# Thirteen of 31 taps of one channel chunk of a depthwise convolution, moved from VectorE to GpSimd

## The chip, the cores and the metric

The kernel runs on one core of a Trainium2 chip. The metric is device time in microseconds (us) of one execution, the median over several runs. In the profile the engines are called PE (TensorE), DVE (VectorE), ACT (ScalarE), POOL (GpSimd) and SP (SyncE, here a queue of transfers).

## The reference: what is computed

Two networks run one after the other on 256 tokens of width 1024, in float32. The change touches the first one alone, in both of its layers (`DEPTH = 2`). Each layer projects its normed input into three branches, runs the branches, concatenates, projects out, and then goes through a large expert block. The branches:

```python
y_att  = forgetting_attention(q, k, v, log_f)      # 8 heads of 64
y_conv = conformer_conv(proj[..., C0:C1], ...)     # 256 channels
y_rnn  = rglru_block(...)
mixed  = concatenate([y_att, y_conv, y_rnn]); x = x + mixed @ w_out[l]
```

The convolution branch gates its input (`a * sigmoid(gate)`), convolves every channel by itself along the tokens with 31 taps (causal: token t sees t-30 to t), adds a bias, takes a layer norm over the 256 channels of each token, and applies SiLU. The second network needs six modulation vectors per layer, `silu(cond) @ mod_w + mod_b`: 24 MB of weights per layer, of which the kernel computes the products early, in the first network's layers.

## The kernel before, in words

Data lie with features on the 128 partitions and tokens along the free dimension, so the convolution's 256 channels are two chunks c = 0 and 1 of 128 partitions by 256 tokens. Everything of this kind (`yconv`, `ypad`, `sqc`, `cen`, scores, probabilities) lives in one big tile that the profile calls `arena`; the constants, tap weights among them, are in `K`, vectors of scalars in `col`. Every float32 product of the big matrices is done as high and low parts: ACT rounds a weight tile (line 1143), DVE takes the rest (L1613), and PE multiplies. Each engine runs its own program in the order of the code and meets the others by semaphores.

**A layer's mixer on DVE.** While PE projects (20 weight tiles), DVE puts taps 0 to 17 of the convolution, both chunks, between its other work. A tap is one instruction (L1766 in `conv`): the padded input shifted by j times the tap's weight, plus `yconv` so far, written to `yconv`; so each tap of a chunk waits for the tap before it. Then comes the loop over attention heads (h = 0 to 8). For head h DVE adds biases to the scores (L1838, L1840), takes maxima (L1844, L1845), and for head g = h-1 divides ACT's exponentials by their sums (L1850 to L1852, which sets `p_ready`), and then does two taps of both chunks, `taps(18 + 2 * g, 20 + 2 * g)`, four instructions (two in g = 6, where only tap 30 is left). After g = 6 it sets `conv_done`.

**The head loop on PE** (from L706 on). At step h it makes the scores of head h+1, the value product of head h-2 and the transposes of head h-1, the last of which wait for `p_ready`. At h = 1, 3 and 5 it also does modulation blocks 7, 8 and 9 (`mod_block`, L622 on; PE rows `bank<-HA,csp`, 32 matmuls in four pieces of 8). At h = 8 it waits for `conv_done` and sums `yconv` over the channels (`bank<-arena,K`, 4 records of 128x256). DVE, ACT and PE then take turns at the layer norm and SiLU; beside that PE does modulation block 10; and then the out-projection begins, whose first weight tile needs the convolution's output last (a wait for DVE's L1829).

**The modulation weights on POOL.** A block of modulation needs four transfers of 512 KB (48 per layer, numbered j; block b uses j = 4b to 4b+3). POOL issues them in order (L2308) into four slots; transfer j may start when PE has used the piece that lay in its slot, that is piece j-4 (`after(pool, S("mod_mm"), ...)`). So the transfers of block 8 start as the pieces of block 7 are used, and so on. In this stage POOL does nothing else. Later, in the expert block, POOL takes the low parts of some tiles (L2296), and between the networks it adds up squares of the context in three additions of 128x1024, 128x512 and 128x256 (L2317), each of which waits for the one before.

Of the kernel before, what the change touches and what calls it, by code (L numbers as in the profile page):

```python
# [12 lines left out]
ALU = mybir.AluOpType  # L13
# [7 lines left out]
T = 256  # L21
# [3 lines left out]
TAPS, RTAPS = 31, 4  # L25
# [37 lines left out]
MODS = [(0, 7), (7, 10), (10, 12)]  # L63
MOD_HEADS = {1: 7, 3: 8, 5: 9}
MSLOT = 4


U_POOL = 18
# [175 lines left out]
def after(eng, sem, value):  # L244

    if not isinstance(value, int) or value > 0:
        eng.wait_ge(sem, value)  # L247
# [17 lines left out]
def build(nc, wts, mod_d, cst_d, keys_d, mla_d, bias_d, x_d, ctx_d, out_d, stop_after=None):  # L265
    ctx = ExitStack()
    with ctx:
# [5 lines left out]
        def S(name):  # L273

            if name not in sems:
                sems[name] = ctx.enter_context(nc.semaphore(name))
            return sems[name]
# [33 lines left out]
        def k(name, a=0, b=None):  # L311
            at, w = CONST[name]
            return K[:, at + a:at + (w if b is None else b)]
# [20 lines left out]
        cvA, cvG, yconv, cen, sqc = (area(2, T) for _ in range(5))  # L334
        ypad, rpad = area(2, T + TAPS - 1), area(2, T + RTAPS - 1)
# [174 lines left out]
        def _(pe):  # L510
# [137 lines left out]
            for l in range(L):  # L648
# [57 lines left out]
                for h in range(HEADS + 2):  # L706
                    if h + 1 < HEADS:
                        head_scores(h + 1)
                    if h < 2:
                        keep_clock(4 + h, bank[3])  # L710
                    if h >= 2:
                        g = h - 2
                        po, hc = slice(64 * (g % 2), 64 * (g % 2) + 64), g // 2
                        pe.wait_ge(S("pt_ev"), HEADS * l + g + 1)
                        if hc >= 2:
                            pe.wait_ge(S("y_ev"), 4 * l + hc - 1)
                        yb = bank[hc % 2]
                        mm(yb[po, 0:T], vtok[:, 0, g * HD:(g + 1) * HD], PT[g % 2][:, 0:T], True, False)
                        mm(yb[po, P:T], vtok[:, 1, g * HD:(g + 1) * HD], PT[g % 2][:, T:3 * P], False, True)\
                            .then_inc(S("pv_mm"), 1)  # L720
                    if 1 <= h <= HEADS:
                        g = h - 1
                        pe.wait_ge(S("p_ready"), HEADS * l + g + 1)
                        if g >= 2:
                            pe.wait_ge(S("pt_ev"), HEADS * l + g - 1)
                        for i in range(3):
                            m = nc.tensor.transpose(bank[6 + g % 2][:, i * P:(i + 1) * P], Pm[g % 2][:, i * P:(i + 1) * P], ident)
                        m.then_inc(S("pt_mm"), 1)
                    if h in MOD_HEADS:
                        mod_block(l, MOD_HEADS[h])  # L730
                    if h == HEADS:
                        pe.wait_ge(S("conv_done"), l + 1)
                        pe.wait_ge(S("y_ev"), 4 * l + 3)
                        for c in range(2):
                            m = mm(bank[0][:, 0:T], k("ones"), yconv[:, c, :], c == 0, c == 1)
                        m.then_inc(S("ln_sum"), 1)
                    if h == HEADS + 1:
                        pe.wait_ge(S("ln_sq"), l + 1)
                        for c in range(2):
                            m = mm(bank[0][:, 0:T], k("ones"), sqc[:, c, :], c == 0, c == 1)  # L740
                        m.then_inc(S("ln_var"), 1)
# [177 lines left out]
            for l in range(L):  # L919
# [13 lines left out]
                if l == 0:  # L933
                    for i in range(16):
# [9 lines left out]
                        j = i - 3  # L944
# [5 lines left out]
                    for o in range(16):  # L950
# [11 lines left out]
                        if o - 1 in MLA_AT:  # L962
                            j = MLA_AT.index(o - 1)
# [3 lines left out]
                        if o - 3 in MLA_AT:  # L967
                            j = MLA_AT.index(o - 3)
# [51 lines left out]
                else:  # L1020
                    for i in range(24):
# [13 lines left out]
                        j = i - 3  # L1035
# [544 lines left out]
        def _(dve):  # L1580
# [139 lines left out]
            for l in range(L):  # L1720
# [33 lines left out]
                lo(t0 + 5 + LEAD)  # L1754
                dve.wait_ge(S("proj_ev"), N_EV * l + 6)

                def conv(out, src, taps, w, b, span, last):

                    for j in span:
                        for c in range(2):  # L1760
                            if j == 0:
                                last[c] = link(v.tensor_scalar(out[:, c, :], src[:, c, 0:T], w[:, c * taps:c * taps + 1],
                                                               b[:, c:c + 1], ALU.mult, ALU.add))
                            else:
                                dve.wait_ge(S("dve_order"), last[c])
                                last[c] = link(v.scalar_tensor_tensor(  # L1766
                                    out=out[:, c, :], in0=src[:, c, j:j + T], scalar=w[:, c * taps + j:c * taps + j + 1],
                                    in1=out[:, c, :], op0=ALU.mult, op1=ALU.add))
# [3 lines left out]
                dve.wait_ge(S("dve_order"), ends[1])  # L1772
                dve.nop().then_inc(S("xr_ready"), 1)

                def taps(a, b):

                    conv(yconv, ypad, TAPS, k(f"cw{l}"), k(f"cb{l}"), range(a, min(b, TAPS)), ends)

                def gate_bias(i):

# [41 lines left out]
                gate_bias(3)  # L1822
                mod_add(l, *MODS[0])
                dve.wait_ge(S("bc_ev"), 5 * (l + 1))
                def mix_low(p):

                    cs = MIX_PARTS[p]
                    dve.wait_ge(S("h_hi"), SPLITS[f"m{l}"][0] + p + 1)
                    v.tensor_tensor(Hl[:, cs[0]:cs[-1] + 1, XS], mixT[:, cs[0]:cs[-1] + 1, :], Hh[:, cs[0]:cs[-1] + 1, XS],  # L1829
                                    ALU.subtract).then_inc(S("h_out"), 1)  # L1830

                for h in range(HEADS + 1):
                    if h < HEADS:
                        dve.wait_ge(S("att_mm"), HEADS * l + h + 1)
                        if h >= 2:
                            dve.wait_ge(S("att_exp"), HEADS * l + h - 1)
                        s_, b = sc[h % 2], bank[4 + h % 2]
                        v.scalar_tensor_tensor(out=s_[:, 0:P], in0=b[:, 0:P], scalar=cT[:, 0, h:h + 1],  # L1838
                                               in1=biasT[:, h, 0:P], op0=ALU.add, op1=ALU.add)
                        v.scalar_tensor_tensor(out=s_[:, P:], in0=b[:, P:3 * P], scalar=cT[:, 1, h:h + 1],  # L1840
                                               in1=biasT[:, h, P:], op0=ALU.add, op1=ALU.add).then_inc(S("att_sc"), 1)
                        dve.wait_ge(S("att_sc"), HEADS * l + h + 1)
                        nm = col[:, 8 + 2 * (h % 2):10 + 2 * (h % 2)]
                        v.tensor_reduce(nm[:, 0:1], s_[:, 0:P], AXX, ALU.max, negate=True)  # L1844
                        v.tensor_reduce(nm[:, 1:2], s_[:, P:], AXX, ALU.max, negate=True).then_inc(S("att_mx"), 1)  # L1845
                    if h >= 1:
                        g = h - 1
                        dve.wait_ge(S("att_exp"), HEADS * l + g + 1)
                        sm = col[:, 12 + 2 * (g % 2):14 + 2 * (g % 2)]
                        seq(v.reciprocal(sm, sm))  # L1850
                        v.tensor_scalar(Pm[g % 2][:, 0:P], Pm[g % 2][:, 0:P], sm[:, 0:1], None, ALU.mult)
                        v.tensor_scalar(Pm[g % 2][:, P:], Pm[g % 2][:, P:], sm[:, 1:2], None, ALU.mult)\  # L1852
                            .then_inc(S("p_ready"), 1)
                        taps(18 + 2 * g, 20 + 2 * g)
                        if g == 6:
                            dve.wait_ge(S("dve_order"), ends[1])
                            dve.nop().then_inc(S("conv_done"), 1)
                        if g == HEADS - 1:
                            dve.wait_ge(S("ln_sum"), l + 1)
                            for c in range(2):  # L1860
                                m = v.scalar_tensor_tensor(out=cen[:, c, :], in0=bank[0][:, 0:T], scalar=-1.0 / 256,
                                                           in1=yconv[:, c, :], op0=ALU.mult, op1=ALU.add)
                            m.then_inc(S("ln_cen"), 1)
                    if h == 7:
                        mix_low(0)
# [420 lines left out]
        def _(pool):  # L2286
# [16 lines left out]
            for l in range(L):  # L2303
                after(pool, S("acc_done"), l)
                for j in range(4 * MODB):
                    n = 4 * MODB * l + j
                    after(pool, S("mod_mm"), n - MSLOT + 1)
                    pool.dma_start(mslot[n % MSLOT], mod_d[n].rearrange("p (a b) -> p a b", a=4)).then_inc(S(f"mod_in{n % MSLOT}"), 16)  # L2308
                pool.wait_ge(S("h_out"), SPLITS[f"m{l}"][1])
                pool.dma_start(keysT.rearrange("p a b -> p (a b)"), keys_d[l]).then_inc(S("keys_in"), 16)  # L2310
                rests(l)
# [31 lines left out]
```

## Time and profile before

| | |
|---|---|
| median of 3 runs | 3182.95 us (3178.98 to 3203.91) |
| profiled execution | 3179.1 us, its span 3177.3 us |
| granted TensorE clock, mean | 0.993 of full speed |
| PE busy | 3111.9 us, 98% of the span |
| DVE busy | 2145.9 us, 68% |
| ACT busy | 1384.7 us, 44% |
| POOL busy | 253.2 us, 8% |

Span is from the first to the last instruction. Busy shares are means over stages of very different kinds: an engine with 68% over the span can be without a gap in the stage that is changed, and one that is 98% busy can be waiting in it between short matmuls. Layer 0's head loop lies from about 116.4 to 146.8 us from the start of the span, layer 1's 1016.7 us later.

### The profile page before, as it was taken

The page shows a single profiled execution, that of the slowest core. Times are in us where ns is not written, and L with a number is a line of the kernel's source. Part 1 is how long each engine was busy: PE and PEld are TensorE (multiplying, and loading weights), DVE is VectorE, ACT ScalarE, POOL GpSimd, SP SyncE. Part 2 cuts the span into 40 slices and gives each one's busy share as a digit, 9 for nine tenths or more (in the row PEclk, how much of TensorE's full clock was granted, in tenths as well). Part 3 has the DMA queues.
Part 4 walks back from the last instruction along what each step waited for, and adds up shares of the span by engine and source line. Part 5 has one row for each costly group of instructions (what it writes and reads, how often), then busy time and mean ns, then how long its engine had stood idle before and what let it go on. Part 6 is the DMA issues. An engine that isn't in the chain of part 4 may idle for free. (4 is left out here: it accounts for less than half of the span.)

```text
span 3177.3 us, 61840 instructions
## 1 busy us (share of the span) xinstructions
PE 3111.9 (98%) x23030; PEld 2705.6 (85%) x23030; DVE 2145.9 (68%) x4315; ACT 1384.7 (44%) x2179; POOL 253.2 (8%) x191
## 2 busy tenths in 40 slices
PE   7999999999999999999999999999999999999999
PEld 6699998989878869998898988876678888875899
DVE  6768876867895767886686898666542234667445
ACT  4544444353444444534444344544532233435444
POOL 1245000000000226400000000000000000000000
PEclk9999999999999999999999999999999999999999
DMA  7745555454445764545545445420022232321354
GB/s 275 245 158 175 166 168 178 158 192 159 158 167 193 258 238 138 195 158 179 173 159 196 150 159 175 160 98 29 1 73 98 95 105 95 107 86 47 120 186 153
DMA packets 131749, 478.46 MB, mean 151 GB/s; under 512 B 14576, under 2 KB 16624, under 8 KB 131056
## 3 DMA queue, kind: packets, MB, share of 16 engines
q1 hardware_dynamic: 115760, 416.72, 38.8%
q0 software_dynamic: 15808, 59.25, 5.5%
q8 instruction: 122, 2.00, 0.2%
q14 instruction: 59, 0.48, 0.0%
HBM read 474.87 MB, written 1.05 MB: 150 GB/s over the span
## 5 line engine op out<-in xcount | busy, mean ns | idle before, releaser
L1613 DVE TENSOR_TENSOR Wl<-ring,Wh 128x1024 fp32r<-128x1024 f32 x720 | 881.7, 1226 | 721.1 <-ACT Wh L1143 718.5
L512 PE MATMUL bank<-HR,Wh 128*128 128x256 f32 (+1 forms) x7488 | 1145.7, 303 | 3.1 <-DVE HR L1829 1.9
L1143 ACT CAST Wh<-ring 128x1024 fp32r<-128x1024 f32 x788 | 823.7, 1046 | 612.6 <-PE bank L512 604.0
L512 PEld LDWEIGHTS bank<-HR,Wh 128*128 128x128 f32 x7488 | 1007.9, 190 | 63.0 <-issue 13.3
L512 PE MATMUL bank<-HR,Wl 128*128 128x256 f32 (+1 forms) x3744 | 609.2, 299 | 0.3 <-DVE Wl L1613 0.3
L512 PE MATMUL bank<-Wh,HR 128*128 128x512 f32 x2304 | 579.4, 394 | 2.8 <-DVE HR L2019 2.8
L512 PEld LDWEIGHTS bank<-HR,Wl 128*128 128x128 f32 x3744 | 523.3, 191 | 23.0 <-DVE Wl L1613 0.5
L512 PEld LDWEIGHTS bank<-Wh,HR 128*128 128x128 f32 x2304 | 426.8, 188 | 94.9 <-issue 5.5
L512 PE MATMUL bank<-arena 128*128 128x32 f16 (+5 forms) x5128 | 362.3, 214 | 18.5 <-issue 5.6
L512 PEld LDWEIGHTS bank<-arena 128*128 128x128 f16 (+3 forms) x5128 | 252.1, 113 | 115.1 <-issue 38.1
L1377 ACT ACTIVATE arena<-bank 128x256 f32 (+1 forms) x256 | 98.4, 385 | 477.9 <-PE bank L512 477.7
L512 PE MATMUL bank<-Wl,HR 128*128 128x512 f32 x1152 | 305.9, 389 | 0.0
L512 PEld LDWEIGHTS bank<-Wl,HR 128*128 128x128 f32 x1152 | 216.2, 188 | 45.2
L1995 DVE TENSOR_TENSOR arena<-arena 128x1024 f16<-128x1024 f16 x256 | 175.1, 684 | 0.1
L2296 POOL TENSOR_TENSOR Wl<-ring,Wh 128x1024 fp32r<-128x1024 f32 x68 | 164.1, 2420 | 99.9 <-ACT Wh L1143 99.7
L2308 POOL DMA_DIRECT2D HA<-mods x96 | 71.9, 755 | 964.3 <-PE bank L512 954.2
L2003 DVE TENSOR_TENSOR arena<-arena 128x256 f16<-128x256 f16 x512 | 126.4, 288 | 25.1 <-DVE arena L1998 1.0
L512 PE MATMUL bank<-FR,Wh 128*128 128x512 f32 (+1 forms) x704 | 129.8, 337 | 0.0
L512 PEld LDWEIGHTS bank<-FR,Wh 128*128 128x128 f32 x704 | 109.6, 190 | 13.7
L2019 DVE TENSOR_TENSOR HR<-arena,HR 128x256 fp32r<-128x256 f32 x256 | 109.1, 429 | 3.0 <-ACT HR L1325 2.8
L2013 DVE TENSOR_TENSOR arena<-arena,bank 128x256 f32 (+1 forms) x256 | 106.0, 414 | 6.1 <-PE bank L512 6.1
L1325 ACT CAST HR<-arena 128x256 fp32r (+1 forms) x256 | 102.1, 402 | 15.7 <-DVE arena L2013 15.7
(247 smaller groups left out, 2013.0 us busy)
## 6 DMA issues: line engine op xcount, KB each, us to landing
ring<-weights SPq DMA_DIRECT2D x788, 512.0 KB, 3.3
HA<-mods POOLq DMA_DIRECT2D x96, 512.0 KB, 6.8
arena<-bias POOLq DMA_DIRECT2D x16, 256.0 KB, 2.9
arena<-keys POOLq DMA_DIRECT2D x2, 1024.0 KB, 6.9
arena<-mla POOLq DMA_DIRECT2D x1, 1536.0 KB, 6.4
K<-constants SPq DMA_DIRECT2D x1, 1402.0 KB, 5.7
X<-x SPq DMA_DIRECT2D x1, 1024.0 KB, 8.2
X<-context POOLq DMA_DIRECT2D x1, 1024.0 KB, 9.0
```

Of the source, the lines that this page charges most:

```text
L512: return nc.tensor.matmul(out, lhsT, rhs, start=first, stop=last)
L1143: nc.scalar.copy(Wh[:, i % SPL], ring[:, i % RAW]).then_inc(S("hi_done"), 1)
L1325: nc.scalar.copy(Hh[:, s % MV, 0:T], GH[q % 2][:, bass.ds(it * R + s, 1), :] .rearrange("p o t -> p (o t)")).then_inc(S("mv_hi"), 1)
L1377: nc.scalar.activation(o, bank[s % 2][:, 0:T], ACT.Gelu_apprx_tanh).then_inc(S("h_ev"), 1)
L1613: v.tensor_tensor(Wl[:, i % SPL], ring[:, i % RAW], Wh[:, i % SPL], ALU.subtract).then_inc(S("lo_done"), 1)
L1995: v.tensor_tensor(Aoh[s % 2], pairs(if12h[:, 0, at]).broadcast_to([P, BT // 2, P, 2]), iotar.unsqueeze(1).broadcast_to([P, BT // 2, P, 2]) ...
L2003: m = v.tensor_tensor(Bg[s % 2][:, part], Boh[s % 2], pairs(gpart[:, part, at]).broadcast_to([P, BT // 2, EQ, 2]), ALU.mult)
L2013: v.tensor_tensor(g, g, bank[2 + s % 2][:, 0:BT * EQ].rearrange("p (t e) -> p e t", t=BT), ALU.mult).then_inc(S("gm_ev"), 1)
L2019: v.tensor_tensor(Hl[:, s % MV, 0:T], GH[q % 2][:, bass.ds(it * R + s, 1), :] .rearrange("p o t -> p (o t)"), Hh[:, s % MV, 0:T], ALU.subt ...
L2296: nc.gpsimd.tensor_tensor(Wl[:, i % SPL], ring[:, i % RAW], Wh[:, i % SPL], ALU.subtract)\
L2308: pool.dma_start(mslot[n % MSLOT], mod_d[n].rearrange("p (a b) -> p a b", a=4)).then_inc(S(f"mod_in{n % MSLOT}"), 16)
```

## The change

In both layers DVE does taps 18 to 30 in the head loop for chunk 0 alone. The same taps of chunk 1 are done by POOL, each as two instructions: a `tensor_scalar` product of the shifted input and the tap's weight into a half of `sqc`, and a `tensor_tensor` addition of that to `yconv`. POOL waits for its own product ahead of each addition (`pool_product`) and for the addition before ahead of each product (`pool_tap`). These pairs stand in the queue of the modulation transfers: taps 18 to 21 behind the issue of j = 31, 22 to 25 behind j = 35, 26 to 30 behind j = 39. Ahead of the first, POOL waits for a new semaphore, `taps_half`, which DVE sets just before the head loop. PE waits at h = 8 for POOL's last addition too. DVE's `conv_done` now hangs on chunk 0's last tap.

```diff
+TAPS_AT = {31: (18, 22), 35: (22, 26), 39: (26, 31)}
...
                         pe.wait_ge(S("conv_done"), l + 1)
+                        pe.wait_ge(S("pool_tap"), (TAPS - 18) * (l + 1))
                         pe.wait_ge(S("y_ev"), 4 * l + 3)
...
-                def conv(out, src, taps, w, b, span, last):
+                def conv(out, src, taps, w, b, span, last, chunks=(0, 1)):
                     for j in span:
-                        for c in range(2):
+                        for c in chunks:
...
-                def taps(a, b):
-                    conv(yconv, ypad, TAPS, k(f"cw{l}"), k(f"cb{l}"), range(a, min(b, TAPS)), ends)
+                def taps(a, b, chunks=(0, 1)):
+                    conv(yconv, ypad, TAPS, k(f"cw{l}"), k(f"cb{l}"), range(a, min(b, TAPS)), ends, chunks)
...
                 dve.wait_ge(S("bc_ev"), 5 * (l + 1))
+                dve.wait_ge(S("dve_order"), ends[1])
+                dve.nop().then_inc(S("taps_half"), 1)
...
-                        taps(18 + 2 * g, 20 + 2 * g)
+                        taps(18 + 2 * g, 20 + 2 * g, (0,))
                         if g == 6:
-                            dve.wait_ge(S("dve_order"), ends[1])
+                            dve.wait_ge(S("dve_order"), ends[0])
                             dve.nop().then_inc(S("conv_done"), 1)
...
                     pool.dma_start(mslot[n % MSLOT], mod_d[n]...).then_inc(S(f"mod_in{n % MSLOT}"), 16)
+                    if j in TAPS_AT:
+                        a, b = TAPS_AT[j]
+                        if a == 18:
+                            pool.wait_ge(S("taps_half"), l + 1)
+                        for t in range(a, b):
+                            after(pool, S("pool_tap"), (TAPS - 18) * l + t - 18)
+                            nc.gpsimd.tensor_scalar(sqc[:, t % 2, :], ypad[:, 1, t:t + T], k(f"cw{l}", TAPS + t, TAPS + t + 1),
+                                                    None, ALU.mult).then_inc(S("pool_product"), 1)
+                            pool.wait_ge(S("pool_product"), (TAPS - 18) * l + t - 17)
+                            nc.gpsimd.tensor_tensor(yconv[:, 1, :], yconv[:, 1, :], sqc[:, t % 2, :], ALU.add).then_inc(S("pool_tap"), 1)
```

## Rows read from the trace of the kernel before

**Rows 1.** The page, busy time, share of the span and instructions of each engine.
```profile
PE 3111.9 (98%) x23030; PEld 2705.6 (85%) x23030; DVE 2145.9 (68%) x4315; ACT 1384.7 (44%) x2179; POOL 253.2 (8%) x191
```
**Rows 2.** Windows, both head loops: length, engines busy (instructions), PE clock, DMA share, GB/s.
```profile
116.40:146.80 30.40, 27.08 (x206) 15.04 (x207) 26.62 (x83) 14.11 (x46) 8.95 (x12) 0.94 0.81 269
1133.10:1163.50 30.40, 26.74 (x203) 14.69 (x204) 26.67 (x83) 14.08 (x46) 9.05 (x12) 0.94 0.76 259
```
**Rows 3.** Timeline of DVE, layer 0's head loop: start, us, operation [idle before <-releaser].
```profile
126.53 0.34 DVE L1838 SCALAR_TENSOR_TENSOR arena<-bank,arena 128x128 f32<-128x128 f32 x1
...
128.02 0.28 DVE L1851 TENSOR_SCALAR arena<-arena,col 128x128 f32<-128x128 f32 x1
128.22 0.35 DVE L1852 TENSOR_SCALAR arena<-arena,col 128x256 f32<-128x256 f32 x1
128.48 1.67 DVE L1766 SCALAR_TENSOR_TENSOR arena<-arena,K 128x256 f32<-128x256 f32 x4
...
134.44 0.35 DVE L1838 SCALAR_TENSOR_TENSOR arena<-bank,arena 128x128 f32<-128x128 f32 x1 [0.73 <-PE bank L512]
...
141.86 0.35 DVE L1838 SCALAR_TENSOR_TENSOR arena<-bank,arena 128x128 f32<-128x128 f32 x1
...
143.83 0.88 DVE L1766 SCALAR_TENSOR_TENSOR arena<-arena,K 128x256 f32<-128x256 f32 x2
```
**Rows 4.** Groups by line, DVE, layer 0's head loop: count, busy us, mean ns.
```profile
L1766 DVE SCALAR_TENSOR_TENSOR arena<-arena,K 128x256 f32<-128x256 f32 x26 | 10.8, 476 | 0.0
```
**Rows 5.** Timeline of PE: ends of blocks 7 to 9, channel sums, block 10, out-projection.
```profile
124.66 0.64 PE L512 MATMUL bank<-HA,csp 128*32 128x256 f32 x8 [0.81 <-DMA HA<-mods]
...
132.91 0.64 PE L512 MATMUL bank<-HA,csp 128*32 128x256 f32 x8 [0.68 <-DMA HA<-mods]
...
140.34 0.64 PE L512 MATMUL bank<-HA,csp 128*32 128x256 f32 x8 [0.32 <-DMA HA<-mods]
...
146.75 1.03 PE L512 MATMUL bank<-arena,K 128*128 128x256 f32 x4
...
151.14 1.93 PE L512 MATMUL bank<-HA,csp 128*32 128x256 f32 x32
...
157.72 0.74 PE L512 MATMUL bank<-HR,Wh 128*128 128x256 f32 x4 [0.96 <-DVE HR L1829]
...
1150.11 0.64 PE L512 MATMUL bank<-HA,csp 128*32 128x256 f32 x8 [0.73 <-DMA HA<-mods]
```
**Rows 6.** Timeline of POOL: issues of transfers j = 28 to 43 of layer 0.
```profile
113.38 2.98 POOL L2308 DMA_DIRECT2D HA<-mods  x4 [13.36 <-PE bank L512]
123.26 3.12 POOL L2308 DMA_DIRECT2D HA<-mods  x4 [6.90 <-PE bank L512]
131.22 2.23 POOL L2308 DMA_DIRECT2D HA<-mods  x3 [4.85 <-PE bank L512]
133.88 0.75 POOL L2308 DMA_DIRECT2D HA<-mods  x1 [0.42 <-PE bank L512]
139.48 2.98 POOL L2308 DMA_DIRECT2D HA<-mods  x4 [4.85 <-PE bank L512]
```
**Rows 7.** Window of 2 us behind those transfers, columns as in rows 2.
```profile
148.00:150.00 2.00, 1.29 (x7) 0.91 (x6) 0.58 (x3) 1.39 (x3) 0.00 (x0) 1.00 0.02 8
```
**Rows 8.** Groups by line, POOL: two of its three additions, mean ns, idle before.
```profile
L2317 POOL TENSOR_TENSOR arena<-arena 128x256 f32<-128x256 f32 x1 | 1.6, 1597 | 0.1
L2317 POOL TENSOR_TENSOR arena<-arena 128x512 f32<-128x512 f32 x1 | 1.4, 1357 | 0.1
```
**Rows 9.** Timelines of POOL (its 128x512 and 128x256 additions) and DVE beside them.
```profile
2017.69 3.03 POOL L2317 TENSOR_TENSOR arena<-arena 128x512 f32<-128x512 f32 x2
...
2015.27 2.63 DVE L2019 TENSOR_TENSOR HR<-arena,HR 128x256 fp32r<-128x256 f32 x1
2017.82 2.31 DVE L1613 TENSOR_TENSOR Wl<-ring,Wh 128x1024 fp32r<-128x1024 f32 x1
2020.05 0.95 DVE L2019 TENSOR_TENSOR HR<-arena,HR 128x256 fp32r<-128x256 f32 x1
...
2022.07 0.41 DVE L2019 TENSOR_TENSOR HR<-arena,HR 128x256 fp32r<-128x256 f32 x1
```

More of the change, by code:

```diff
@@ L2308, in _ @@
                     pool.dma_start(mslot[n % MSLOT], mod_d[n].rearrange("p (a b) -> p a b", a=4)).then_inc(S(f"mod_in{n % MSLOT}"), 16)
+                    if j in TAPS_AT:
[7 more added lines that the diff above has]
+                            pool.wait_ge(S("pool_product"), (TAPS - 18) * l + t - 17)
+                            nc.gpsimd.tensor_tensor(yconv[:, 1, :], yconv[:, 1, :], sqc[:, t % 2, :], ALU.add)                                .then_inc(S("pool_tap"), 1)
                 pool.wait_ge(S("h_out"), SPLITS[f"m{l}"][1])
```

## The prediction

> **What bounds the kernel now.** The page first: PE is busy for 98% of the span, DVE for 68%, POOL for 8% [rows 1]. That speaks for giving POOL work, but the means hide the stage that is changed, so next I read windows of the two head loops. There DVE is busy 26.6 of 30.4 us and PE 27.1, and the transfers run at 0.81 and 0.76 of their engines [rows 2]. DVE's timeline then shows what a head costs: 126.53 to 130.15 for one, 3.6 us, of which the four taps are 1.67 us [rows 3]. Up to h = 7 DVE has few gaps. One stands out: 0.73 us at 134.44, ended by PE [rows 3]. So the question is what PE waited for, and PE's timeline answers it: the last piece of block 7 waited 0.81 us for a transfer of modulation weights, that of block 8 0.68, that of block 9 0.32, and layer 1's block 8 0.73 [rows 5]. POOL's timeline closes the ring: the transfers of block 8 are issued from 123.26, just as block 7's pieces are used, those of block 9 from 131.22 and 133.88, as block 8's are [rows 6]. From the first issue to the use of the last piece is 132.91 - 123.26 = 9.65 us for block 8 and 140.34 - 131.22 = 9.1 us for block 9. Two things therefore hold the loop at the same pace, some 7 to 8 us per two heads: DVE's work, and the ring of transfers through POOL's queue. The change makes the first shorter and puts work into the second.
>
> **What it takes from DVE.** 26 taps of 0.476 us cost 10.8 us per layer, overlapped by a little [rows 4]. Thirteen go. The two left per head are both of chunk 0 and each needs the one before, so I cost them at two full 0.48, 0.96 in place of 1.67: 0.7 saved per head in six heads, and 0.88 less 0.48 = 0.4 at the end, 4.6 us per layer. How much of it reaches the end? Until block 9 nothing: PE takes blocks 7, 8 and 9 in its order, each already ended by its transfer, so an earlier `p_ready` only makes PE wait longer there. Behind block 9 (140.98) come the scores of head 7, which DVE takes up at 141.86 [rows 3] as soon as PE has made them; the taps of g = 5 end ahead of that and their saving becomes idle time. Only the last 0.4 remains. DVE's new signal ahead of the loop waits for a tap long done: nothing, behind the biases that the loop needs anyway.
>
> **What a pair costs on POOL.** POOL's three additions give the price. The 128x512 one took 1.357 us, the 128x256 one 1.597 [rows 8], which makes no sense by size. The second view explains it: DVE's subtraction of 128x256, 0.41 us when alone, took 2.63 beside them and ended at 2017.90; DVE's 1.23 us subtraction took 2.31 and ended at 2020.13; POOL's last addition ended at 2020.72 [rows 9]. The two engines took turns: an addition of 128x256 needs 0.59 us once DVE is out of the way, and up to 1.60 with the turn. A product of this form is not in the trace; I take 0.59 for it too, the same width on the same engine, and 1.60 as its upper end, 0.3 (half, for one input where the addition has two) as its lower. Between dependent additions lie 0.07 us (1.357 from 2017.69 ends at 2019.05, and 3.03 less 1.597 starts the next at 2019.12) [rows 8, 9]. A pair alone is 0.59 + 0.59 + 0.14 = 1.32 us. Beside the loop DVE takes its turns: per head two taps, 0.96, and I also count L1851 and L1852, 0.28 + 0.35 [rows 3], though no row here shows that these two exclude POOL. One head's worth, 1.59, falls on a burst of four pairs: 5.28 + 1.59 = 6.9 us, 1.72 a pair; five pairs 8.6.
>
> By the Trainium skill ("SBUF — State Buffer", "Who interferes with whom") a `tensor_scalar` in a 2-port mode contends with GpSimd as an instruction with two SBUF inputs does; by that both kinds count, and without it a burst would be 0.6 us shorter. Its "GPSIMD Engine Reference" (4.1) says that one-input operations run there at roughly line rate; an estimate of 256 cycles at 1.2 GHz, 0.21 us, would make the pair 0.94, the sum below 0.5 + 0.6 a layer, and the time 3185; no row here has such an operation.
>
> **Where the pairs stand.** The first burst begins when j = 31 is issued, 113.38 + 2.98 = 116.36 [rows 6], call it 116.5 with the signal, and DVE's competing operations come only from 120.9 on; it ends between 121.8 and 123.4. The next issue was at 123.26: **nothing**. The second burst begins behind j = 35, 126.38, and ends at 133.25. Transfers of block 9 used to start at 131.22: **2.0 us late**. They land as long after their first issue as before, 9.1 us, so block 9 ends 2.0 us late, and with it everything behind it on PE. The third burst begins at 133.25 + 2.98 and ends at 144.85; j = 40 was issued at 139.48, so block 10's transfers start 5.4 late. That is covered: they had landed by 148.0 (the DMA share is 0.02 behind it) [rows 7], block 10's last piece is used at 152.4 (151.14 + 1.93 - 0.64) [rows 5], and block 10 itself moves by 2.0, which makes 6.4 us. If that cover goes, each us is a us of path, less the 0.96 that PE waits in the first out-projection tile [rows 5]. PE's new wait for the last addition, at 144.85, is hidden too: the channel sums would be at 146.75 + 2.0. Behind it on PE would stand the norm, block 10 and the out-projection.
>
> **DVE waiting for POOL.** DVE's four operations per head each meet a POOL operation in flight, and wait for 0 to 0.59 us. Ahead of block 9 the ring covers most of that: 4 x 0.3 less the saved 0.7 is 0.5 a head, against the 2.0 given. Behind block 9 one head's operations still meet the third burst: 1.0 us.
>
> **Sum.** Per layer 2.0 + 1.0 - 0.4 = 2.6, twice 5.2. The profiled execution took 3179.1, 3.85 less than the median 3182.95; against it 3184.3, as a median 3188.
>
> **Rivals.** *The ring does not bind* (0.13): if transfers get quicker once the queue is spread, or pairs are near 1.2 us, DVE's 4.6 per layer may come through in part: 3174 at best, 3182 if just nothing happens. For it: DVE's loop has almost no gap. Against: three blocks out of three end in a wait for a transfer. *DVE becomes the bound* (0.15): if each of the four operations waits for a whole POOL operation, that is 2.4 a head, less 0.7 saved, 1.7 in the six heads beside the bursts, 10 per layer: 3203. It decides where the mean wait passes about 0.4 us, for then two heads add 2 x (1.7 - 0.7) = 2.0 us, as much as the ring gives. The 2.63 us subtraction speaks for it, that POOL pauses for its own semaphores and its issues against. *POOL's queue becomes the bound* (0.07), the slower side: with a pair of c us the three bursts and the two issue groups between them put j = 40 at 116.5 + 13c + 6.1; less 139.48, the 4.4 us of cover and 0.96 at the out-projection, the layer is 13c - 22.2 us late. At the upper end, c = 3.34, that is 21 a layer and 3225; it passes 1% at c = 2.9. The 1.597 row is for it; against, that this row holds a turn of a 1.2 us DVE operation, and nothing in the loop is longer than 0.48. The forecast itself has 0.65.
>
> **Numbers.** Most likely 3188. Low end 3176: most of the DVE saving of both layers, 2 x 3.5. High end 3207: c = 2.4 gives 9 a layer, 3201, and some lock waits on top; it takes in the DVE rival and leaves out slow POOL. A measurement of this kernel can tell about 1%, 32 us, from no change. Faster by that is beyond any case (the whole saving is 9 us): 0.01. Slower is POOL's queue as the bound: 0.07. Within: 0.92.
>
> **What would show it.** In the changed profile: DVE's L1766 with 13 records in each loop; POOL with 52 new records in both layers, products and additions of 128x256 near 0.6 us, some to 1.1; POOL's issue behind the second burst near 133 in place of 131.22; a wait of PE for a transfer ahead of block 9 of about 2 us more, and none ahead of block 10; DVE's gaps wider ahead of h = 5 and 6; DVE's L1851, L1852 and taps longer where POOL works. I am wrong if the loop ends earlier than before, if a product costs much more than the addition, if PE waits for POOL at the channel sums, or if PE's clock falls in the out-projection because it has waited longer.

## The result, and the profile after

The changed kernel takes 3200.43 us (median of 20 runs, 3195.33 to 3203.90); the kernel before, in 20 runs beside it, 3189.11 (3178.98 to 3203.91). The ratio is 1.0030 with a 95% interval of 1.0019 to 1.0042: about 9.6 us slower (6 to 13), within the 1% that I called no change. The forecast was 3188, the range 3176 to 3207. In two of the runs below, one execution at a far lower mean clock (0.555 and 0.785) is left out of the medians, means and ratios. The profiled execution took 3198.55, its span 3196.7. That is 19.4 us over the profiled span of before, twice what the 20 runs show: the traced execution of before (3179.1) is among its fastest. The traces show where time goes in this pair; how much it is in the mean, the runs say.

The busy shares, set against [rows 1], say little: DVE has 26 instructions less (4289), POOL 52 more (243), PE is busy for 98% as before.

POOL's timeline, first layer 0, then layer 1, is to be read beside [rows 6]: start, us, operation, [idle before].

```profile
114.47 2.98 POOL L2312 DMA_DIRECT2D HA<-mods  x4 [13.37 <-PE bank L513]
117.57 0.93 POOL L2319 TENSOR_SCALAR arena<-arena,K 128x256 f32<-128x256 f32 x1
118.58 0.72 POOL L2322 TENSOR_TENSOR arena<-arena 128x256 f32<-128x256 f32 x1
119.41 0.92 POOL L2319 TENSOR_SCALAR arena<-arena,K 128x256 f32<-128x256 f32 x1
...
124.93 3.06 POOL L2312 DMA_DIRECT2D HA<-mods  x4
128.02 0.94 POOL L2319 TENSOR_SCALAR arena<-arena,K 128x256 f32<-128x256 f32 x1
129.05 0.88 POOL L2322 TENSOR_TENSOR arena<-arena 128x256 f32<-128x256 f32 x1
...
135.46 3.04 POOL L2312 DMA_DIRECT2D HA<-mods  x4
...
148.23 3.04 POOL L2312 DMA_DIRECT2D HA<-mods  x4
...
1138.40 2.96 POOL L2312 DMA_DIRECT2D HA<-mods  x4 [13.37 <-PE bank L513]
...
1148.77 2.30 POOL L2312 DMA_DIRECT2D HA<-mods  x3
...
1160.95 3.31 POOL L2312 DMA_DIRECT2D HA<-mods  x4 [1.20 <-PE bank L513]
```

Before, every issue had idle time ahead of it, ended by PE. In layer 0 the three issues behind the bursts now have none: POOL comes to them straight from an addition. From the issue of j = 28 to that of j = 32, 36 and 40 it is now 10.46, 20.99 and 33.76 us, where [rows 6] give 9.88, 17.84 and 26.10: 0.6, 3.2 and 7.7 us late. In layer 1 the first burst holds j = 32 by about as much (10.37 us behind j = 28), but ahead of j = 36 POOL stands idle for 1.20 us and waits for PE: there the second burst holds nothing back.

PE's timeline, first layer 0, then layer 1, is to be read beside [rows 5].

```profile
125.77 0.64 PE L513 MATMUL bank<-HA,csp 128*32 128x256 f32 x8 [0.70 <-DMA HA<-mods]
...
134.45 0.64 PE L513 MATMUL bank<-HA,csp 128*32 128x256 f32 x8 [0.68 <-DMA HA<-mods]
135.02 1.71 PE L513 MATMUL bank<-arena 64*128 64x128 f32 x8
...
141.84 0.64 PE L513 MATMUL bank<-HA,csp 128*32 128x256 f32 x8 [1.15 <-DMA HA<-mods]
143.35 0.64 PE L513 MATMUL bank<-HA,csp 128*32 128x256 f32 x8 [0.87 <-DMA HA<-mods]
144.72 1.08 PE L513 MATMUL bank<-HA,csp 128*32 128x256 f32 x8 [0.73 <-DMA HA<-mods]
145.73 3.12 PE L513 MATMUL bank<-arena 64*128 64x128 f32 x8
...
155.36 1.91 PE L513 MATMUL bank<-arena,K 128*128 128x256 f32 x4
...
160.63 1.93 PE L513 MATMUL bank<-HA,csp 128*32 128x256 f32 x32
...
167.22 0.74 PE L513 MATMUL bank<-HR,Wh 128*128 128x256 f32 x4 [0.96 <-DVE HR L1833]
...
1148.76 0.64 PE L513 MATMUL bank<-HA,csp 128*32 128x256 f32 x8 [1.04 <-DMA HA<-mods]
1150.30 0.64 PE L513 MATMUL bank<-HA,csp 128*32 128x256 f32 x8 [0.90 <-DMA HA<-mods]
...
1159.54 3.64 PE L513 MATMUL bank<-HA,csp 128*32 128x256 f32 x32
...
1172.36 3.42 PE L513 MATMUL bank<-HA,csp 128*32 128x256 f32 x32
...
1181.56 1.03 PE L513 MATMUL bank<-arena,K 128*128 128x256 f32 x4
...
1192.53 0.74 PE L513 MATMUL bank<-HR,Wh 128*128 128x256 f32 x4 [0.97 <-DVE HR L1833]
```

The kernel before has in layer 1: the issue of j = 28 on POOL, and on PE the last pieces of blocks 7 and 9, the channel sums and the first out-projection tile.

```profile
1130.09 2.98 POOL L2308 DMA_DIRECT2D HA<-mods  x4 [13.36 <-PE bank L512]
...
1141.25 0.64 PE L512 MATMUL bank<-HA,csp 128*32 128x256 f32 x8 [0.70 <-DMA HA<-mods]
...
1157.37 0.64 PE L512 MATMUL bank<-HA,csp 128*32 128x256 f32 x8 [0.15 <-DMA HA<-mods]
...
1163.79 1.03 PE L512 MATMUL bank<-arena,K 128*128 128x256 f32 x4
...
1174.76 0.74 PE L512 MATMUL bank<-HR,Wh 128*128 128x256 f32 x4 [0.97 <-DVE HR L1829]
```

Two things are to be seen. Block 9 of layer 0 waits 2.75 us for three of its four pieces, where before it waited 0.32 for one. And a few records take nearly twice as long from there: eight matmuls of 64x128 take 3.12 us at 145.73 and 1.71 at 135.02, a whole block 3.64 and 3.42 where block 10 takes 1.93. Windows of those stretches (columns as in [rows 2]) give the reason, PE's clock at 0.53, nearly all of it, some 14 and 24 us, at 1.2 GHz in place of 2.4:

```profile
144.72:159.00 14.28, 12.92 (x42) 7.03 (x43) 4.54 (x14) 4.59 (x12) 6.27 (x8) 0.53 0.43 148
1150.50:1175.80 25.30, 25.30 (x133) 14.73 (x125) 13.14 (x36) 7.15 (x24) 21.94 (x27) 0.53 0.51 170
```

Before, PE was at 0.57 in the first 4 us of layer 0's loop, ahead of block 7, and at 1.00 from 120 us on, through all its waits for transfers:

```profile
116.00:120.00 4.00, 3.60 (x14) 1.51 (x14) 2.04 (x7) 0.73 (x4) 0.36 (x1) 0.57 0.96 323
```

In layer 0 the way from the issue of j = 28 to the last wait of the first out-projection tile is 52.75 us, before 44.34: 3.3 of the 8.4 us are lost up to block 9's last piece (30.25 for 26.96), 4.2 from there to the channel sums (10.64 for 6.41), 0.9 behind. In layer 1 it is 54.13 for 44.67, 9.5 us more, all of it by the end of block 9: behind that the two kernels take the same 5.78 to the sums and 10.97 to the tile. The loops account for 17.9 of the 19.4 us between the two profiled executions.

In layer 0 the trace shows the whole chain: late issues, late transfers, PE's waits in block 9, then half clock. In layer 1 it does not. There the clock fell right behind block 7, whose last two pieces waited 1.04 and 0.90 us for transfers that were issued at 1138.40, ahead of the first burst. Blocks 8 and 9 then ran at half clock without a wait for a transfer. What made block 7 wait longer there (0.70 us for one piece before) these rows do not show.

DVE's group of taps in layer 0, against [rows 4]: 13 taps, as intended, but each 0.61 us in the mean. The second row is the longest wait of DVE in that loop, for the scores of head 7. POOL's groups, both layers, follow.

```profile
L1768 DVE SCALAR_TENSOR_TENSOR arena<-arena,K 128x256 f32<-128x256 f32 x13 | 7.9, 608 | 0.2
...
147.42 0.35 DVE L1842 SCALAR_TENSOR_TENSOR arena<-bank,arena 128x128 f32<-128x128 f32 x1 [5.60 <-PE bank L513]
```

```profile
L2319 POOL TENSOR_SCALAR arena<-arena,K 128x256 f32<-128x256 f32 x26 | 25.8, 993 | 2.3
L2322 POOL TENSOR_TENSOR arena<-arena 128x256 f32<-128x256 f32 x26 | 19.3, 741 | 2.2
```

### The profile page after: what moved, and what is told of

Same layout as the page of the kernel before. It is cut to its first block and busy times, and to the rows that moved or that the text cites. A ratio compares the mean times of both kernels' runs of the same rounds, so it can differ in the third digit from the quotient of the medians.

```text
span 3196.7 us, 61861 instructions
## 1 busy us (share of the span) xinstructions
PE 3126.7 (98%) x23030; PEld 2712.6 (85%) x23030; DVE 2141.5 (67%) x4289; ACT 1383.8 (43%) x2179; POOL 298.1 (9%) x243
## 5 line engine op out<-in xcount | busy, mean ns | idle before, releaser
L513 PE MATMUL bank<-arena 128*128 128x32 f16 (+5 forms) x5128 | 369.1, 216 | 18.5 <-issue 5.6
```

Of the source, the lines that this page charges most:

```text
L513: return nc.tensor.matmul(out, lhsT, rhs, start=first, stop=last)
```

## The experiments

The theory: **POOL's queue**. A burst holds back the issues behind it, PE waits for transfers, and then PE's **clock** falls, which costs more than the wait. Rivals: **the lock** (DVE's operations wait for POOL's and DVE sets the pace), and **freed DVE** (DVE runs ahead, PE's work comes in bursts, and the clock falls of that). Times are set against runs of the kernel before on the same chip (medians 3187 to 3189).

**Only POOL's part** (`e1_pool_added`).

```diff
-                        taps(18 + 2 * g, 20 + 2 * g, (0,))
+                        taps(18 + 2 * g, 20 + 2 * g)
-   nc.gpsimd.tensor_tensor(yconv[:, 1, :], yconv[:, 1, :], sqc[:, t % 2, :], ALU.add)
+   nc.gpsimd.tensor_tensor(th[:, 1, :], th[:, 1, :], sqc[:, t % 2, :], ALU.add)
```

> DVE keeps all taps of both chunks as in the kernel before; POOL does its 26 pairs at the same places in its queue, the sum into a scratch area that nothing reads. Queue theory (the pairs, 1.85 us each in the changed kernel's trace, hold back the transfers behind them, and PE's clock falls because PE waits): as slow as the changed kernel, 8 to 13 us over the kernel before, block 9's last piece over 25 us from the issue of j = 28 in both layers. Lock theory (DVE's two-input operations wait for POOL's and the loop runs at DVE's pace): clearly slower than the changed kernel, since DVE now has 4.6 us more per layer and twice as many taps that meet POOL: 18 to 30 us over before. Freed-DVE theory (the clock falls because DVE runs ahead and PE's work comes in bursts): within 4 us of before.

Measured: 3196.61, ratio 1.0030 (1.0016 to 1.0043). The whole loss comes with POOL's work alone; that DVE drops 13 taps adds nothing that can be told. Freed DVE is not needed for the loss, and the lock's 18 to 30 us did not come either, though the lock is there: DVE's 26 taps take 0.63 us each, and PE once waits 1.61 us for DVE. The groups of DVE and a row of PE:

```profile
L1768 DVE SCALAR_TENSOR_TENSOR arena<-arena,K 128x256 f32<-128x256 f32 x26 | 14.9, 631 | 0.0
```

```profile
133.75 0.55 PE L728 MATMUL bank<-K,arena 128*128 128x128 f32 x3 [1.61 <-DVE arena L1856]
```

Block 9's last piece in layer 0 lies 30.3 us behind the issue of j = 28, against 26.96 before and 30.25 in the changed kernel; the 25 us of the expectation were no test, since before is above them too.

**Only DVE's part** (`e2_dve_freed`).

```diff
-                        for t in range(a, b):
-                            ... product and addition on POOL
+                        pass
-                        pe.wait_ge(S("pool_tap"), (TAPS - 18) * (l + 1))
```

> DVE drops taps 18 to 30 of chunk 1, and POOL does nothing for them: those 13 taps per layer are left out. Queue theory: nothing to hold back the transfers, so the loops stay at the ring's pace: between 2 us under and 1 us over the kernel before, PE's clock in the loops at 0.9 or more. Freed-DVE theory: PE's clock falls in the loops as in the changed kernel, 5 to 10 us over before. If the ring did not bind before (my first rival): up to 9 us under.

Measured: 3190.37, ratio 1.0011 (0.9995 to 1.0027), not to be told from before. My first rival, that the saving comes through, is out: there is no gain with POOL out of the way. The interval does reach to 8.6 us over before, so that a part of the freed-DVE theory's 5 to 10 us is not excluded, and the mean clock of these executions, 0.9897, lies between before (0.9912) and the changed kernel (0.9880). And the expectation on the clock failed in the profiled execution: a window of layer 0's loop has 0.83, where the kernel before has 0.97.

```profile
112.00:162.00 50.00, 44.43 (x315) 26.00 (x314) 28.25 (x83) 23.16 (x59) 13.36 (x18) 0.83 0.57 190
```

So PE may fall to half clock without POOL's work too: here after 2.19 us of waits in three pieces of block 8. One execution does not settle how often.

**The transfers from ACT** (`e3_act_issues`).

```diff
-TAPS_AT = {31: (18, 22), 35: (22, 26), 39: (26, 31)}
+TAPS_AT = {31: (18, 31)}
+  act.wait_ge(S("mod_mm"), 4 * (MODB * l + MOD_HEADS[h - 1] + 1))
+  for j in range(4): act.dma_start(mslot[...], mod_d[n]...)
   mod_evac(l, MOD_HEADS[h - 1])
```

> The changed kernel, but the transfers j = 32 to 43 of each layer are issued by ACT, four at a time when a block's pieces are used, and POOL does its 13 pairs in one run behind j = 31. Queue theory: no pair stands ahead of a transfer; the loops are as in the kernel before or up to 3 us shorter in each layer (transfers from ACT may land sooner), clock 0.9 or more: 0 to 8 us under before. Lock theory: DVE's taps still take 1.0 to 1.6 us per two beside POOL; the loops stay 3 us or more longer in each layer than before.

Measured: 3198.70, ratio 1.0035 (1.0018 to 1.0051). The expectation failed, and the trace says why the test was a bad one. Last pieces of blocks 7, 8 and 9 on PE:

```profile
126.08 0.64 PE L513 MATMUL bank<-HA,csp 128*32 128x256 f32 x8 [0.67 <-DMA HA<-mods]
...
136.11 0.64 PE L513 MATMUL bank<-HA,csp 128*32 128x256 f32 x8 [0.69 <-DMA HA<-mods]
...
145.71 0.64 PE L513 MATMUL bank<-HA,csp 128*32 128x256 f32 x8 [0.74 <-DMA HA<-mods]
```

They lie 10.0 and 9.6 us apart; in [rows 5] 8.25 and 7.43. ACT issues all four when the last piece is used (126.78, 2.71 us, in which ACT's own work stands), POOL issued each as its slot came free. No pair was ahead of a transfer, but the ring was slower by a like amount. It agrees with the ring as the bound and says nothing on the lock.

**Fillers against the fall of the clock** (`e4_clock_kept`).

```diff
+  if 7 <= b < 10 and 2 * half + h:
+      for _ in range(5):
+          mm(bank[3][:, 2 * P:], onesb[:, 0:P], onesb, True, True)
   pe.wait_ge(S(f"mod_in{n % MSLOT}"), 16 * (n // MSLOT + 1))
```

> The changed kernel with 5 filler matmuls of 256 columns (about 0.6 us) ahead of the second, third and fourth piece of blocks 7, 8 and 9, where PE waits for transfers; results go to unused columns. Clock theory (most of the loss is PE at half clock, 10.64 us from block 9 to the channel sums in layer 0 where before had 6.41, and 3 to 4 us records of 8 matmuls in layer 1): granted clock in both loops back to 0.9 or more, block 9 to sums near 6.5 in both layers, 5 to 9 us under the changed kernel, so 1 to 6 over before. If waiting alone costs the time and the clock only shows it: same as the changed kernel within 2 us, or slower by the fillers.

Measured: 3192.77, ratio 1.0022 (1.0011 to 1.0032). Both loops, columns as in [rows 2]:

```profile
116.00:153.00 37.00, 35.46 (x256) 19.27 (x256) 24.87 (x72) 14.75 (x47) 32.43 (x40) 0.91 0.59 194
1140.00:1178.00 38.00, 35.56 (x254) 19.16 (x255) 24.35 (x71) 14.44 (x48) 32.06 (x39) 0.91 0.59 198
```

The clock is held: the 0.91 comes from the first 7 us of each loop, ahead of the fillers, and from 125 to 153 us, and in layer 1 from 1149 to 1178, it is 1.00. The mean over the executions is 0.9926, the changed kernel's 0.9880. From block 9's last piece to the sums it is 6.42 us in both layers, as expected. The time goes the way expected, 6 us over before in place of 11 by the medians; but the two intervals overlap, so the gain is likely and not shown. What is left may be the late transfers and the fillers themselves; this run does not part them.

**POOL writes but does not read** (`e6_memsets`).

```diff
-  nc.gpsimd.tensor_scalar(sqc[:, t % 2, :], ypad[:, 1, t:t + T], ...)
+  nc.gpsimd.memset(arena[:, 6210:7234], 0.0)
-  nc.gpsimd.tensor_tensor(yconv[:, 1, :], yconv[:, 1, :], sqc[:, t % 2, :], ALU.add)
+  nc.gpsimd.memset(arena[:, 6210:6978], 0.0)
```

> The changed kernel with each product and addition of POOL replaced by a memset of 1024 and 768 columns of an unused area, about as long, with the same waits; chunk 1 has no taps 18 to 30, and POOL reads nothing. Queue theory: if the bursts are as long as in the changed kernel, the transfers are as late and the time is the same: 8 to 13 us over before. Lock theory: DVE's taps no longer wait (0.48 each, two in 1.0 us, in place of 1.4 to 1.6), and the time falls to that of the run with DVE freed alone, 1 to 5 over before.

Measured: 3198.17, ratio 1.0035 (1.0023 to 1.0047): the same loss. POOL's issues behind the bursts and DVE's taps in layer 0:

```profile
127.51 3.00 POOL L2312 DMA_DIRECT2D HA<-mods  x4
...
137.83 2.97 POOL L2312 DMA_DIRECT2D HA<-mods  x4
```

```profile
L1768 DVE SCALAR_TENSOR_TENSOR arena<-arena,K 128x256 f32<-128x256 f32 x13 | 6.2, 478 | 0.2
L1855 DVE TENSOR_SCALAR arena<-arena,col 128x128 f32<-128x128 f32 x8 | 3.7, 457 | 0.3
L1856 DVE TENSOR_SCALAR arena<-arena,col 128x256 f32<-128x256 f32 x8 | 3.6, 453 | 0.0
```

The issues are 10.3 us apart as in the changed kernel (10.5), the taps are back at 0.478 us, and the time does not move: taking the lock from DVE's taps gains nothing. By itself this does not tell queue and lock apart, for the lock has moved: L1855 and L1856, 0.31 and 0.37 us in the changed kernel, now take 0.46 and 0.45, and with the taps they come to 13.5 us in the loop, there to 13.4. But the chain of layer 0 is seen in both layers of this run: block 9 waits 2.18 and 2.90 us for transfers, and PE is at half clock for some 14 us from there.

**Nine pairs, where POOL is idle** (`e5_spread9`).

```diff
-TAPS_AT = {31: (18, 22), 35: (22, 26), 39: (26, 31)}
+TAPS_AT = {31: (22, 25), 35: (25, 27), 39: (27, 29), 43: (29, 31)}
+                taps(18, 20, (1,))
                 lo(t0 + N_IN - 2 + LEAD)
                 gate_bias(2)
+                taps(20, 22, (1,))
```

> Nine of the thirteen pairs stay on POOL, cut to what fits into its idle time between the issues: three behind j = 31, two each behind 35, 39 and 43 (3.7 us in gaps of 4.85 us). DVE does taps 18 to 21 of chunk 1 ahead of the loop, where it waits for ACT. Queue theory: no issue starts late; waits of PE for transfers as in the kernel before, the time within 3 us of before at equal mean clock; what is left over is the clock. If any POOL work beside the loop costs (lock theory): 4 us or more over before at equal mean clock, as the changed kernel (6) and the run that added POOL's pairs (4.5).

Measured: 3186.30, ratio 1.0003 (0.9987 to 1.0019): the loss is gone. Every issue of POOL in layer 0 has idle time ahead of it again:

```profile
123.44 3.06 POOL L2314 DMA_DIRECT2D HA<-mods  x4 [0.45 <-PE bank L513]
...
130.91 1.57 POOL L2314 DMA_DIRECT2D HA<-mods  x2 [0.57 <-PE bank L513]
...
140.12 3.04 POOL L2314 DMA_DIRECT2D HA<-mods  x4 [1.01 <-PE bank L513]
```

This run also decides on the lock. DVE waits for POOL at least as much as in the changed kernel: in layer 0 its taps take 0.58 us (there 0.61) and its first division (L1857, there L1855) 0.49 (there 0.31). The loss does not come:

```profile
L1768 DVE SCALAR_TENSOR_TENSOR arena<-arena,K 128x256 f32<-128x256 f32 x15 | 8.7, 580 | 0.2
L1857 DVE TENSOR_SCALAR arena<-arena,col 128x128 f32<-128x128 f32 x8 | 3.9, 491 | 0.3
```

Place and number of the pairs change together here, and no run has all thirteen in the gaps. A cost that went by the number alone would be 9/13 of 9.6, 6.6 us; the interval ends at 6.1. In layer 1 of this execution PE still fell to half clock for some 14 us, after 2.16 us of waits in block 8, so the fall is not peculiar to long bursts; in the mean the clock is 0.9914, before beside it 0.9912.

**The kernel before with 3 fillers, and the nine pairs with 3 fillers** (`e7_before_fillers`, `e8_spread9_fillers`; the edit of the fillers with `range(3)`).

> The kernel before with 3 filler matmuls of 256 columns ahead of the second, third and fourth piece of blocks 7 to 9. Clock theory: the loops of before lose time too in executions whose mean clock is low (its 33 runs go from 3178 at 0.996 to 3201 at 0.985); with fillers the clock stays at 0.99 or more in every run: 2 to 6 us under before, and runs closer together. If fillers cost as much as they hold: within 2 us; if the clock follows the total and not these loops: same spread as before.

> Nine pairs spread as in the first run of this set, and the 3 fillers. Queue and clock theory together: neither late transfers nor a fall of the clock: within 2 us of the kernel before with fillers. Lock theory: 4 us or more over that.

Measured: 3186.10, ratio 0.9997 (0.9988 to 1.0006), and 3187.09, ratio 1.0003 (0.9992 to 1.0014). The clock is held, 0.9941 and 0.9933 in the mean, and the runs are closer together (3182 to 3192 and 3184 to 3192, before 3180 to 3199), but the time is that of before: by this the fillers cost about what they hold. Between the two runs nothing is left of the lock at this resolution.

**Later blocks: three heads per turn of the ring** (`e9_before_late`; with the nine pairs as three, three and three, `e10_spread_late`; and with fillers, `e11_spread_late_fillers`).

```diff
-MOD_HEADS = {1: 7, 3: 8, 5: 9}
+MOD_HEADS = {1: 7, 4: 8, 7: 9}
```

> The kernel before with modulation blocks 8 and 9 at h = 4 and 7 in place of 3 and 5, so that the ring of transfers has three heads per block (10.6 us of DVE's time at 3.55 a head) in place of two, against the 9.1 to 9.65 us that it needs. Ring theory: PE no longer waits for transfers of blocks 8 and 9, the 0.3 to 0.9 us per block come back, and the clock falls less: 1 to 5 us under before. If the ring did not hold the loop: within 1 us, or slower where block 10 now waits for its transfers.

> The nine pairs on POOL (three each behind j = 31, 35 and 39; DVE does taps 18 to 21 of chunk 1 ahead of the loop) and blocks 8 and 9 at h = 4 and 7. If it was the ring alone that kept DVE's saving from coming through: the loop now goes at DVE's pace, about 2.9 us a head, and is 1 to 2.5 us shorter per layer than before: 2 to 5 us under the kernel before with late blocks, 3 to 8 under before. If DVE's waits for POOL take the saving, or PE's clock falls because DVE no longer holds PE in step: no better than the kernel before with late blocks.

> The kernel of the run ahead of this one with the 3 filler matmuls ahead of the second to fourth pieces of blocks 7 to 9. Clock theory: mean clock 0.992 or more and runs closer together; faster than the same without fillers if its clock falls (by up to 4 us), slower by the fillers (up to 3) if it does not.

Measured: 3189.37, 3186.84 and 3187.80, ratios 1.0001 (0.9987 to 1.0015), 1.0002 (0.9985 to 1.0019), 1.0002 (0.9990 to 1.0014). None differs from before. With late blocks PE's waits for transfers at blocks 8 and 9 are gone, but others stand in their place; in the second of these runs PE's rows in layers 0 and 1 show

```profile
143.28 0.55 PE L728 MATMUL bank<-K,arena 128*128 128x128 f32 x3 [1.28 <-DVE arena L1858]
...
1174.50 0.64 PE L513 MATMUL bank<-HA,csp 128*32 128x256 f32 x8 [0.77 <-DMA HA<-mods]
```

a wait for DVE, whose pairs of taps take 1.0 to 1.6 us beside POOL, and one of block 10 for its transfers. Neither expectation of the ring theory is borne out, though the intervals leave room for 4 to 5 us: with the ring relieved the kernel before gains nothing that can be told (PE waits 1.56 us for DVE at 143.65), and the nine pairs give the outcome put down for DVE's waits taking the saving. A head costs DVE 3.1 to 3.5 us in that run (three heads from 131.03 to 140.99), not 2.9. So the ring was not alone in holding the loop, and where DVE holds it the lock may count. No version ran clearly faster than the kernel before.

**The clock of all executions.** Each execution gives its mean granted clock. Over 93 of the kernel before the time falls by 2.2 us for each 0.001 (3201 us at 0.985, 3178 at 0.996). The changed kernel's 20 have 0.9880 in the mean, before 0.9912: by that line some 7 us. At equal mean clock it is 5.4 us slower (0.5 standard error), POOL's part alone 3.8, the memsets 4.5, the transfers from ACT 6.1, DVE's part alone -0.4, the nine pairs 1.3 (these 0.5 to 0.8). With 3 fillers the kernel before lies 4.7 over this line and the nine pairs 4.5. This goes by correlation; only the fillers are an intervention on the clock.

## Why the prediction was right, and what in it was off

- **What bounds the loop** held as put: two things at the same pace. A shorter DVE gains nothing: DVE's part alone is not faster than before, and the changed kernel's DVE stands idle 5.60 us for head 7's scores. A relieved ring alone gains nothing that can be told either (later blocks, 1.0001): PE then waits for DVE.
- **A pair on POOL** was mis-sized. I took 0.59 for product and addition, 1.32 us for a pair alone and 1.72 with DVE's turns. The addition takes 0.72 undisturbed (0.64 in the run with POOL's part alone, which adds into another tile, `th`), the product 0.92, a pair alone 1.84 (117.57 to 119.41). The bursts of four took 7.36 and 7.44 us, 1.86 a pair: DVE's turns, put at 1.59 a burst, added 0.1 or 0.2. That 1.72 came near is luck, two misses of opposite sign. The product was the larger miss in price, and dearer than the addition, which I had named as a sign of being wrong: one input does not make it cheaper than two. The Trainium skill ("GPSIMD Engine Reference", 4.1) has one-input operations at roughly line rate; by my estimate from it 0.21 us. The trace does not agree, and the measurement decides.
- **The first burst** was put at nothing and cost 0.6 us. **The second** was put at 2.0; in layer 0 block 9's issues were 3.2 us late by then, the 0.6 among them, and block 9 3.3. In layer 1 it held nothing back. **The third**, 5.4 forecast and 7.7 measured in layer 0, was hidden as said: block 10 has no wait, and PE did not wait for POOL at the sums.
- **DVE waiting for POOL**, 1.0 us per layer behind block 9, failed as a cost. Block 9 came so late that behind it the third burst was over: POOL is at its next issue from 148.23, and head 7's division and tap (149.12 and 149.38) took 0.35 and 0.48 us, as alone. Ahead of block 9 the taps do take longer, 0.61 for 0.476, but DVE waits for PE there, and the nine pairs make it wait as much for POOL without a loss. L1851 and L1852, which I counted among the waiting, did not stretch (0.31 and 0.37, before 0.31 and 0.39). By the Trainium skill ("SBUF — State Buffer", "Who interferes with whom") a DVE instruction with two SBUF inputs contends with a GpSimd one that reads SBUF and not with one that only writes; the trace agrees, 0.608 and 0.478.
- **The clock** is the step that was missing from the sum. I named a fall in the out-projection as a sign of being wrong; it fell in the head loop itself, for 14 us in layer 0 and 24 in layer 1. In this pair of traces it is about half of the loss in layer 0 (4.2 of 8.4 us) and 8.7 of 9.5 in layer 1 (from block 7's last piece to block 9's end 25.5 us, before 16.8). The trace of before had shown 0.94 in both loops [rows 2]. That came from the start of the loop and not from the waits for transfers, so the question I left out is what longer waits would do.
- **The sum** of 5.2 us compares with 9.6 (6 to 13). At equal mean clock it is 5.4, near the forecast, but that is luck: in layer 0 the wait for the second burst was 1.3 us too cheap and the lock 1.0 too dear, and in layer 1 neither term shows in the trace; its loss is nearly all the clock's. Of the 12 us between 3188 and 3200, 6 are the base: the median of before was 3182.95 in three runs and is 3189.11 in 20.
- **Rivals.** The ring not binding, with DVE's saving coming through, is out (DVE's part alone). DVE as the bound is out (the nine pairs; and in the changed kernel DVE waits for PE). POOL's queue as the bound, which I gave 0.07 at the size of 1%, names the right queue but not the path: by its formula 1.86 us a pair would make 2.0 us a layer through the third burst and block 10, and block 10 did not wait. What cost, in layer 0, was the second burst, which the forecast itself had.

## What to carry to other kernels

An engine that is 8% busy may be the one that starts transfers just in time; set work for its queue against the idle time between two issues (here 4.85 us, two pairs), and not against the total: cut to that it cost nothing that could be told, in bursts of 7.4 us 0.3%. Ask of each new wait of PE what it does to the granted clock: here waits of 2.75 and 1.94 us within a block were followed by 14 and 24 us at half clock, while 2.22 us in block 9 of one run (POOL's part alone, layer 0) were not. Ask too whether the traced execution is a usual one: ours of before was among its fastest. And take the base from many executions when the question is a few tenths of a percent.

## What the runs showed of the hardware that I had not expected

- POOL: a product of 128x256 with a scalar per partition takes 0.92 us, an addition of two such tiles 0.72; memsets of 1024 and 768 columns take 0.96 and 0.74.
- DVE's two-input taps stretch from 0.476 to 0.61 us beside POOL's products and additions, and not at all (0.478) beside POOL's memsets. L1855 and L1856 of the changed program, with one SBUF input, stretch beside the memsets, to 0.46 and 0.45 in the mean (before 0.31 and 0.39). In the changed kernel they do not (0.31 and 0.37); with nine pairs the first does (0.49).
- The mean granted clock of the same kernel differs from execution to execution, 0.985 to 0.996, and 23 us go with it.
